# Stick-breaking attention logits: two half-array matmuls become two full-array matmuls with a zero-padded query tile, and the list scheduler gets other costs

## The reference, cut to what matters

```
z = einsum('bhqd,bhkd->bhqk', qb, kb) * scale          # 128 queries against all keys up to them
log_keep = where(mask, log_sigmoid(-z), 0)
suffix = cumsum(log_keep, reverse) - log_keep
weights = where(mask, exp(log_sigmoid(z) + suffix), 0)
out = einsum('bhqk,bhkd->bhqd', weights, vb)
```

## Time and profile before

| | |
|---|---|
| time of the runs, median | 2933.82 us (2933.01 to 3374.3, 3 runs) |
| the profiled execution, its own time | 2921.85 us |
| its span, slowest core (core 5) | 2920.1 us |
| spans of the eight cores | 2896.3 to 2920.1 us |
| mean granted clock, both dies | 0.985 |
| PE matmul busy | 2797.7 us, 96% |
| DVE, ACT, POOL busy | 49%, 43%, 55% |

### The profile page before, as it was taken

How to read it: one execution, slowest core, us unless ns; L and a number is a source line. 1 busy time by engine, 2 the same in 40 slices (tenths; PEclk the granted TensorE clock), 3 DMA queues, 4 the chain that set the end, 5 groups by cost and what they waited for, 6 DMA issues and landing times.

```text
span 2920.1 us, 43942 instructions; the slowest of 8 cores (2896.3 to 2920.1 us)
## 1 busy us (share of the span) xinstructions
PE 2797.7 (96%) x13211; PEld 1194.9 (41%) x13211; DVE 1436.4 (49%) x1759; ACT 1261.6 (43%) x2062; POOL 1602.0 (55%) x1793
## 2 busy tenths in 40 slices
PE   8999999999999999799998999999999989999998
PEld 3444444444443344343443444444444434444443
DVE  4411246464435555776645454445565675554003
ACT  3433234736335344365543353433645464444231
POOL 4655515765417777576761465550576766674333
PEclk9999999999999999899999999999999999999999
DMA  8798883456665999746755344465355485446222
GB/s 171 157 208 196 177 216 90 120 150 147 184 155 107 193 177 175 190 123 157 167 139 155 85 107 113 114 157 170 92 123 123 106 216 135 114 114 184 86 77 83
DMA packets 491478, 420.24 MB, mean 144 GB/s; under 512 B 310128, under 2 KB 334960, under 8 KB 491248
## 3 DMA queue, kind: packets, MB, share of 16 engines
q1 hardware_dynamic: 465184, 370.07, 49.1%
q0 software_dynamic: 26064, 47.36, 11.3%
HBM read 304.23 MB, written 89.13 MB: 135 GB/s over the span
## 4 chain that ended last, share of the span: by engine, by line
PE 79%; DMA 6%; DVE 6%; issue 4%; POOL 3%; ACT 2%; SPq 1%; DVEq 0%; POOLq 0%; ACTq 0%
PE ps L588 74%; PE ps L1349 3%; PE ps L1402 2%; DMA stg<-xT 2%; DMA ring<-wblk 1%; DVE vt L1209 1%; DVE P L1365 1%; DMA h<-xT 1%; POOL Wq L1379 1%; DMA Wk<-Wq 1%; SPq L581 1%; DVE X L746 1%; POOL ps L1064 1%; DMA ring<-wbf 1%; POOL ffB L937 0%
## 5 line engine op out<-in xcount | busy, mean ns | idle before, releaser
L588 PE MATMUL ps<-X,ring 128*128 128x512 bf16 x6144 | 1399.1, 383 | 36.3 <-DVE X L746 11.1
L588 PEld LDWEIGHTS ps<-X,ring 128*128 128x128 bf16 x6144 | 586.0, 98 | 778.9 <-issue 121.5
L1379 POOL TENSOR_TENSOR Wq<-P 128x1024 bf16<-128x1024 f32 (+2 forms) x320 | 529.1, 1655 | 299.3 <-DVE P L1365 289.7
L588 PE MATMUL ps<-mix,ring 128*128 128x512 bf16 x2816 | 657.0, 380 | 7.2 <-POOL P L1360 4.1
L1365 DVE TENSOR_TENSOR_SCAN P<-ps,carry,cbs 128x512 f32<-128x512 f32 x384 | 488.9, 1279 | 346.1 <-POOL P L1360 200.6
L578 ACT ACTIVATE ps<-ps 128x512 f32<-128x512 f32 (+3 forms) x576 | 429.6, 750 | 477.4 <-PE ps L588 238.2
L588 PE MATMUL ps<-ffB,ring 128*128 128x512 bf16 x2048 | 485.1, 380 | 0.0
L811 DVE TENSOR_TENSOR tmp<-ps,ms 128x512 f32<-128x512 f32 x256 | 175.3, 685 | 494.0 <-PE ps L588 493.3
L816 POOL TENSOR_TENSOR h<-tmp,h 128x512 f32<-128x512 f32 x224 | 287.7, 1284 | 229.9 <-DVE tmp L811 229.1
L588 PEld LDWEIGHTS ps<-mix,ring 128*128 128x128 bf16 x2816 | 263.8, 98 | 339.7 <-issue 39.6
L1365 DVE TENSOR_TENSOR_SCAN P<-ps,cbs 128x128 f32<-128x128 f32 (+3 forms) x256 | 208.1, 819 | 323.6 <-ACT ps L578 189.4
(11 more groups left out here) (82 smaller groups left out, 1755.2 us busy)
## 6 DMA issues: line engine op xcount, KB each, us to landing
ring<-wbf SPq DMA_DIRECT2D x540, 256.0 KB, 3.0
ring<-wblk POOLq DMA_DIRECT2D x180, 256.0 KB, 7.9
wbf<-ring SPq DMA_DIRECT2D x180, 256.0 KB, 6.4
stg<-xT SPq DMA_DIRECT2D x96, 256.0 KB, 4.8
h<-xT SPq DMA_DIRECT2D x64, 256.0 KB, 7.4
hsp<-h SPq DMA_DIRECT2D x64, 256.0 KB, 3.7
h<-hsp SPq DMA_DIRECT2D x64, 256.0 KB, 6.2
oT<-mixf SPq DMA_DIRECT2D x32, 256.0 KB, 5.1
```

The costliest lines, as they stand in the source:

```text
L588: ins = pe.matmul(out, lhsT=l, rhs=r, start=(first and i == 0), stop=(last and i == n - 1), skip_group_check=True)
L1379: yield Req("pool", lambda e: e.tensor_tensor(out=W4, in0=P[:, :, 1:w + 1].rearrange("p h (j n) -> p h j n", n=128), in1=P[:, :, 0:w].rear ...
```

## The change

Five things, in one edit of the builder:

1. The logits pair. A new tile `qz` of 2 KB per partition holds a group's 512 queries twice: head 0's channels on partitions 0 to 63 with zeros below, and head 1's on partitions 64 to 127 with zeros above. The zero halves are set once at the start by two POOL memsets. A new fiber `spread_q` copies the two halves from `qT` with two ACT instructions for each group of one `a` and one `tq`. A logits matmul now takes all 128 rows of `kT` and the tile of its head, so that the other head's rows meet zeros. There is one `qz` tile (`p_qz`), given back when the group's last logits pair has been placed, and an item waits for its group's tile.
2. `RING` goes from 10 to 9 slots, which is the room that `qz` takes.
3. The scheduler books 1.28 us when the activation table changes (sigmoid and gelu each their own, logarithm and exponential one together); it books 0.1 us where PE goes to the value matmuls and 0.21 us where it comes back; it lengthens a POOL operation, or a DVE operation that touches no PSUM bank, by its overlap with the other kind.
4. Durations: the logits pair w/1200+0.01 instead of w/2400+0.07; POOL adds 1.29 instead of 1.15, POOL products 1.06 instead of 1.15, logarithm 0.72 instead of 1.3, exponential 0.65 instead of 0.9, and some others.
5. DMA rate 235 instead of 256 KB per us, first-pass loads 470 instead of 456 KB, write-backs 170 instead of 150.

`Sched.ready`, by which the next operation is chosen, and all dependencies outside the logits stay as they are.

```
-RING = 10
+RING = 9
-DMA_KB_US = 256.0
+DMA_KB_US = 235.0
...
@@ Sched.op
-        self.free[eng] = start + r.dur
-        o.fin = start + r.dur
+        if r.tab is not None and r.tab != self.tab:
+            self.tab = r.tab
+            start += 1.28
+        if eng == "pe" and r.mode != self.mode:
+            start += 0.1 if self.mode == 0 else 0.21
+            self.mode = r.mode
+        end = start + r.dur
+        if r.lock:
+            a, b = self.held["dve" if eng == "pool" else "pool"]
+            end += max(0.0, min(b, end) - max(a, start))
+            self.held[eng] = (start, end)
+        self.free[eng] = end
+        o.fin = end
...
@@ Req
+        self.lock = key is None and (eng == "pool" or eng == "dve" and not any(
+            t.name.startswith("bank") for t in writes + reads))
...
+        self.qz = sb("qz", [128, 1, 2, 512], BF16)
...
@@ act
+        q.tab = func if func in (AF.Sigmoid, AF.Gelu) else None
...
@@ ring_fiber, keep_block
-                      kb=256.0 if b in self.Lwbf else 456.0)
+                      kb=256.0 if b in self.Lwbf else 470.0)
...
@@ square
-                [LX[k][t] for k in rows[1]], [LX[k][t] for k in rows[0]], 0.70 if eng == "dve" else 1.15)
+                [LX[k][t] for k in rows[1]], [LX[k][t] for k in rows[0]], 0.72 if eng == "dve" else 1.29)
...
@@ rms
-            [self.Lcf], [self.Lms[ms], self.Lbank[bk]], 1.3)
+                [self.Lcf], [self.Lms[ms], self.Lbank[bk]], 0.72)
+        q.tab = AF.Ln
...
-        yield Req("act", lambda e: e.activation(out=m, in_=m, func=AF.Exp, scale=power), [], [self.Lms[ms]], 0.9)
+        q = Req("act", lambda e: e.activation(out=m, in_=m, func=AF.Exp, scale=power), [], [self.Lms[ms]], 0.65)
+        q.tab = AF.Ln
...
@@ evac_h
-            eng, d = ("dve", 0.70) if last and c >= 6 else ("pool", 1.15)
+            eng, d = ("dve", 0.71) if last and c >= 6 else ("pool", 1.29)
...
@@ attention
         yield lambda: self.qkn == 24
+        for a in range(4):
+            for tq in range(2):
+                self.M.spawn(self.spread_q(a, tq, items), 0.0)
...
+    def spread_q(self, a, tq, items):
+        z = yield self.p_qz
+        ts = slice(tq * TT, (tq + 1) * TT)
+        for h in range(2):
+            hp = slice(h * 64, (h + 1) * 64)
+            yield Req("act", (lambda h, hp: lambda e: e.activation(out=self.qz[hp, z, h, :], in_=self.qT[hp, a, ts], func=AF.Copy))(h, hp),
+                      [self.LqT[a][tq], self.Lqz0], [self.Lqz[z]], 0.64)
+        mine = [x["g"]["st"] for x in items if x["g"]["a"] == a and x["g"]["tq"] == tq]
+        mine[0]["z"] = z
...
@@ att_item
+        yield lambda: "z" in st
+        qz, Lqz = self.qz[:, st["z"]], self.Lqz[st["z"]]
...
-                hp = slice(h * 64, (h + 1) * 64)
-                ins = pe.matmul(zt[:, h * 512:h * 512 + w], lhsT=self.qT[hp, a, il * 128:(il + 1) * 128],
-                                rhs=self.kT[hp, a, k0:k0 + w], start=True, stop=True, skip_group_check=True)
+                ins = pe.matmul(zt[:, h * 512:h * 512 + w], lhsT=qz[:, h, r * 128:(r + 1) * 128],
+                                rhs=self.kT[:, a, k0:k0 + w], start=True, stop=True, skip_group_check=True)
-        yield Req("pe", zmm, [self.LqT[a][tq], self.LkT[a][c]], Lz, w / 2400.0 + 0.07, bias=-0.04, wslack=0.5)
+        yield Req("pe", zmm, [Lqz, self.LkT[a][c]], Lz, w / 1200.0 + 0.01, bias=-0.04, wslack=0.5)
+        st["zn"] = st.get("zn", 0) + 1
+        if st["zn"] == 4 * st["nch"]:
+            self.p_qz.free(st["z"])
...
-                      0.15 + 0.216 * (2.5 if first else 4), bias=-0.04, slack=4.0)
+                      0.15 + 0.216 * (2.5 if first else 4), bias=-0.04, slack=4.0, mode=2)
```

More of the change, by code:

```diff
@@ L59, in __init__ @@
         self.dma_free = 0.0
+        self.tab = None
+        self.mode = 0
+        self.held = {"pool": (0.0, 0.0), "dve": (0.0, 0.0)}
     def alias(self, new_lts, old_lts):
@@ L197, with __init__ @@
 class Req:
-    __slots__ = ("eng", "fn", "reads", "writes", "key", "dur", "lat", "bias", "kb", "slack", "wslack")
-    def __init__(self, eng, fn, reads, writes, dur, key=None, lat=0.0, bias=0.0, kb=256.0, slack=0.0, wslack=0.0):
+    __slots__ = ("eng", "fn", "reads", "writes", "key", "dur", "lat", "bias", "kb", "slack", "wslack", "tab", "mode", "lock")
+    def __init__(self, eng, fn, reads, writes, dur, key=None, lat=0.0, bias=0.0, kb=256.0, slack=0.0, wslack=0.0, mode=0):
         self.eng = eng
@@ L211, in __init__ @@
         self.wslack = wslack
+        self.tab = None
+        self.mode = mode
+        self.lock = key is None and (eng == "pool" or eng == "dve" and not any(
+            t.name.startswith("bank") for t in writes + reads))
 class Pool:
@@ L536, in alloc @@
         self.Lao = lst("ao", 2)
+        self.Lqz = lst("qz", 1)
+        self.Lqz0 = LT("const")
+        self.p_qz = Pool(range(1))
         self.LCY, self.LCC = lst("cy", 3), lst("cc", 3)
@@ L577, in act @@
         dur = ((172 if psum else 224) + n) / 1.2e3 + 0.03
-        return Req("act", lambda e: e.activation(out=out, in_=in_, func=func, **kw), reads, writes, dur, bias=bias)
+        q = Req("act", lambda e: e.activation(out=out, in_=in_, func=func, **kw), reads, writes, dur, bias=bias)
+        q.tab = func if func in (AF.Sigmoid, AF.Gelu) else None
+        return q
     def dma(self, out, in_, reads, writes, key, kb=256.0):
@@ L634, in keep_block @@
     def keep_block(self, slot, b):
-        yield self.dma(self.wbf[b], self.ring[:, slot, :], [self.Lring[slot]], [self.Lwbf[b]], ("keep", slot), kb=150.0)
+        yield self.dma(self.wbf[b], self.ring[:, slot, :], [self.Lring[slot]], [self.Lwbf[b]], ("keep", slot), kb=170.0)
         self.busy.discard(slot)
@@ L689, in square @@
             yield Req("pool", lambda e: e.tensor_tensor(out=Xf[:, SQ[i][odd], hs], in0=sq, in1=sq, op=ALU.mult), Ls,
-                          [LX[k][t] for k in rows[odd]], 1.15, bias=0.5)
+                          [LX[k][t] for k in rows[odd]], 1.06, bias=0.5)
         else:
@@ L721, in rms @@
         m = self.ms[:, ms, :]
-        yield Req(
-            "act", lambda e: e.activation(out=m, in_=self.bank(bk), func=AF.Ln, scale=1.0 / D,
-                                          bias=self.cf[:, 60:61]),
-            [self.Lcf], [self.Lms[ms], self.Lbank[bk]], 1.3)
+        q = Req("act", lambda e: e.activation(out=m, in_=self.bank(bk), func=AF.Ln, scale=1.0 / D, bias=self.cf[:, 60:61]),
+                [self.Lcf], [self.Lms[ms], self.Lbank[bk]], 0.72)
+        q.tab = AF.Ln
+        yield q
         self.banks.free(bk)
-        yield Req("act", lambda e: e.activation(out=m, in_=m, func=AF.Exp, scale=power), [], [self.Lms[ms]], 0.9)
+        q = Req("act", lambda e: e.activation(out=m, in_=m, func=AF.Exp, scale=power), [], [self.Lms[ms]], 0.65)
+        q.tab = AF.Ln
+        yield q
         return ms
@@ L937, in evac @@
                     yield Req("pool", lambda e: e.tensor_tensor(out=F[:, jj, ts], in0=m, in1=m, op=ALU.mult),
-                              [self.Ltmp[b]], [LF[jj][t]], 1.15)
+                              [self.Ltmp[b]], [LF[jj][t]], 1.06)
                     self.p_tmp.free(b)
@@ L1065, in evac @@
                     out=S1[:, b0:528][:, ::-1], in0=src[:, b0:528][:, ::-1], in1=src[:, b0 - d:528 - d][:, ::-1],
-                    op=ALU.add))(src, d, b0), [Ls], [L1], 1.15)
+                    op=ALU.add))(src, d, b0), [Ls], [L1], 1.07)
                 src, Ls = S1, L1
@@ L1074, in evac @@
                 out=PB[:], in0=S1[:, 16:528], scalar=1.0 / wdw, in1=A[:, 16:528], op0=ALU.mult, op1=ALU.subtract),
-                [LA], [L1], 1.25)
+                [LA], [L1], 0.72)
             if seq0:
@@ L1310, in attention @@
                 nch = u * 2 + tq + 1
-                st = dict(left=nch)
+                st = dict(left=nch, nch=nch)
                 prev = [None] * 4
@@ L1337, in att_item @@
         a, c, first, end, tq, st = G["a"], G["c"], G["first"], G["end"], G["tq"], G["st"]
-        il = tq * 4 + r
+        yield lambda: "z" in st
+        qz, Lqz = self.qz[:, st["z"]], self.Lqz[st["z"]]
         zs = yield self.zsets
@@ L1464, in setup @@
         yield Req("dve", lambda e: e.memset(self.cb[:, 128:640], 0.0), [], [self.Lz0], 0.3)
+        for h in range(2):
+            yield Req("pool", (lambda h: lambda e: e.memset(self.qz[(1 - h) * 64:(2 - h) * 64, :, h, :], 0.0))(h), [],
+                      [self.Lqz0], 0.8)
         yield self.dma(self.cf[:], self.cf_d, [], [self.Lcf], "cf", kb=72.0)
```

## The result

The changed kernel takes **2956.8 us** in the median of its runs, against 2933.82 before: a ratio of **1.0066, interval 1.0043 to 1.0089**. (The ratio leaves out executions in the chip's slower state: it sets 2950.8 to 2956.8 us against 2933.0 to 2933.8.) It is slower by 0.7%, where the forecast was 2906 us and 1.0% faster, and it lies above the range. Run again in the first session of the experiments, on one chip with the other kernels, it had 1.0056 (1.0025 to 1.0087). So a loss of 0.4 to 0.6% is what has to be explained.

What follows compares the result with a forecast made beforehand. PE, busy for 96% of the span, was taken as the bound. Pair -5, refill +4, ring +4 and order -31 give -28 us: 2894 on the profiled execution, 2906 us as the median 12 above it; range 2878 to 2950.

Steps and rivals of the forecast that it cites:

- The logits pair: Attention logits on PE: full-array pairs drop 0.215 us of switching but lose the shared exit behind value matmuls; -5 us.
- rival 4: Logits pairs on PE: two full matmuls cost one matmul more and the 0.215 us stays; 58 us, 2992 us; chance 0.04.
- The refill: First logits pair of each of 32 groups: waits for two ACT copies, 1.26 us; 4 us taken, bounds 0 and 40.
- Rival 2: PE stands at each of 32 query-tile refills, 1.26 us plus ACT's lateness; 2973, up to 2995 us; chance 0.12.
- The ring: Weight loads: one slot less keeps one block less in flight; 4 us taken, bounds 0 and 14.
- The order: PE's instruction list: 62 us of waits and lost clock hang on wrong planned times, new costs reach half; -31 us.
- Rival 1: The list is remade but no better, table loads still fall between logarithm and exponential; +3, 2937 us; chance 0.25.
- the 21 us of the clock: Pulses lost to lowered PE clock in four stretches holding the longest waits; 21 us, counted within the order's 62.

Runs made afterwards that it cites:

- Three edits: On the kernel before: late norm's and pooling matmuls placed later (1.0094); first tile's norm started early (0.9995); the same with next-stage residual loads held back (1.0023).
- The two other lists: The changed kernel with the semaphore booked at 0.20 us (1.0023) or 0.16 us (1.0033) in place of 0.18: same instructions, other order.
- SEM = 0.16: The changed kernel with the semaphore booked at 0.16 us in place of 0.18, same instructions in another order: 1.0033.
- the two matmuls placed later: The kernel before with the late norm's matmul placed 10 us behind plan in place of 2, and the pooling matmul 8 in place of 1.5: 1.0094.
- the early norm on the new costs: New scheduler costs, old logits, ten slots; first tile's norm started beside the last MLP groups, next stage's residual loads held for value-projection blocks: 1.0051.

## Why the prediction was wrong, by its own steps

**The logits pair: right in the row, mis-sized in the sum.** The prices after the change are the forecast ones (0.11, 0.22, 0.44 against 0.11, 0.22, 0.43), a pair of 512 keys behind value matmuls went from 0.32 to 0.44 us in the median on core 5 (0.43 was forecast), and the 0.215 us around a pair went away as it said. So rival 4 is out, and the rule for contractions of 64 rows that the prediction quotes from the Trainium skill doesn't hold here as a rule of time: two row tiles save a matmul and pay it back in switching. The sum of -5 us is not seen. Take all steps from one matmul's start to the next, into, inside and out of pairs and value groups, as far as they are under 1 us, so that long waits drop out, less each matmul's own columns. On core 5 in both second profiles they add up to -33.3 us before and -30.6 after: +2.7. One piece of the difference is read off: a pair at 512 keys that stands alone costs 0.435 us in place of 0.421, which over 224 pairs is +3 us, where the prediction had -0.7. Of the rest, how much belongs to pairs that stand two together or next to value groups wasn't taken apart.

**The refill: mis-sized, and rightly bounded.** 4 us taken, none found on PE in the changed kernel. Rival 2 is out by the lists of waits: its price of 1.26 us is met once at most, and not 32 times.

**The ring: mis-sized.** 4 us taken with bounds 0 and 14. Taking the slot costs 0.23% on the old costs, 7 us, and 0.30% on the new ones, and a second slot about as much again. The term was sized by one core's waits for bfloat16 blocks, 3.4 us. What grew are the waits for float32 blocks in the first pass, and they fall unequally: 0 us on two cores and 8.1 us on the slowest of the changed kernel's second profile, and the time is the slowest core's.

**The order: this step failed.** It said that 62 us hang on an order made with wrong times and that the new costs reach half. Both timings of the new costs alone say -0.09%, 3 us, and the waits fell by 1.4 us out of 102.9. Three things were wrong in it. First, a wait in PE's list is not a gain that waits to be taken. Three edits each removed or cut the wait that they aimed at (the squares' 13.3 to 0, line 701's 31 to 18.5, the blocks' 8.3 to 0), and the sum of the waits never fell below the 102.9 of the kernel before (128.4, 104.4, 110.6): other waits took their place. Second, better durations didn't make better places: with them booked, the squares' wait grew in every profile, from 13.3 us to 21 with ten slots and 23 in the changed kernel, and there are more table loads than before (71 and 67 against 61). Rival 1 described this (a new order, no better, with loads still between logarithm and exponential) and had the sum at +3; it was held at one in four. Third, the 21 us of the clock were too many: they count all lost pulses of the four stretches of the earlier trace rows, in which PE was busy for 50.4 of 86 us, and a pulse that is lost while PE stands costs nothing.

**What is left.** Slot 7 us, pairs 3, refill 0, costs -3: that is +7 us, 0.24%. The two other lists of the changed kernel lose 0.23% and 0.33%, its own 0.41% without the execution at a lowered clock and 0.56% with it. So up to 5 us of the loss, or 9 with that execution, have no cause on record. The luck of one list isn't shown to be it: the changed kernel's two long waits, 11 to 12 us for the pooling chain between the first S and the next F and 9.1 us for the squares, stand in the list of `SEM = 0.16` too. What speaks against the sum is that the padded logits cost 0.07% over the slot on the old costs (1.0030 against 1.0023, within both intervals) and 0.40% on the new costs at ten slots; whether the order, the three norm tiles or something else makes this difference stays open. That an order alone can cost 0.6 to 0.9% is shown by two other kernels: the one with the two matmuls placed later (1.0094), and the early norm on the new costs (1.0051 against 0.9991, with loads moved as well). Open, too, is what brings the 0.81 stretches of the first profile.

## What to carry to other kernels

Before you book a wait as a gain, ask what PE meets next; the way to find out is to remove one wait by hand and see whether the sum of the waits falls. Where one engine is 95% busy and the rest is list order, count the buffers that a change takes as part of its price, and take it from the slowest core's row. And compare a re-planned kernel with two or three other lists of the same work, in one session, before you believe 0.3% in either direction.

## What the runs showed of the hardware that I had not expected

A row-tiled pair of matmuls at 512 columns costs 0.42 to 0.43 us with its two switches, and two full-array matmuls cost 0.43 to 0.44: the zero half of the array is free in time. In three profiles, 5.1 to 11.1 us more of PE's waits went with 8.4 to 16.2 us more of time, so the time lost was more than the waits that the list shows. And the granted clock can fall to 0.81 for 2 to 15 us at a time, mostly on one die, within an execution whose mean clock is still 0.97 on the slowest core; there it cost 36 us of pulses.
